# PEER layers as one stage, modulation spread over other stages, attention slots in another order

## What is computed

```python
h = modulate(x, norm_mix_g[l], sh1, sc1)          # RMSNorm, scale, shift
y = mixer_ab(h, ...) if l == 0 else mixer_ssd(h, ...)
x = x + g1 * y
h = modulate(x, norm_ffn_g[l], sh2, sc2)
x = x + g2 * peer_ffn(h, ...)

def peer_ffn(h):                                   # for each token
    q = (h @ wq).reshape(8 heads, 256)             # two halves of 128
    s1, s2 = q[:, :128] @ k1.T, q[:, 128:] @ k2.T  # 128 keys a half
    # top 16 of s1 and of s2, top 16 of their 256 sums -> 16 experts a head
    act = gelu(u_tab[expert] . h);  gate = softmax(best)
    return sum(gate * act * v_tab[expert])         # over 8 heads x 16 experts
```

## Time and profile before

| | us |
|---|---|
| median of 3 runs | 3028.67 |
| lowest, highest | 3025.58, 3033.92 |
| the profiled execution | 3031.45 |
| its span, first to last instruction | 3029.7 |
| PE, DVE busy in it | 2320.6, 1477.1 |
| POOL, ACT busy in it | 905.6, 636.4 |

### The profile page before, as it was taken

How to read it: one execution, slowest core, us unless ns; L and a number is a source line. 1 busy time by engine, 2 the same in 40 slices (tenths; PEclk the granted TensorE clock), 3 DMA queues, 4 the chain that set the end, 5 groups by cost and what they waited for, 6 DMA issues and landing times. The chain is left out here.

```text
span 3029.7 us, 24058 instructions
## 1 busy us (share of the span) xinstructions
PE 2320.6 (77%) x8016; PEld 1271.0 (42%) x8016; DVE 1477.1 (49%) x3612; ACT 636.4 (21%) x1444; POOL 905.6 (30%) x779
## 2 busy tenths in 40 slices
PE   5876678867778777877896879678677877777876
PEld 2543345523333333333675678455433323333333
DVE  0124411177667767763133521411376767766754
ACT  1115412212222222121112211201222222222211
POOL 1203300054444444542002322000144444444441
PEclk8887789989989989998997865589899999999898
DMA  8724627499999999996231034022399999999993
GB/s 330 295 87 188 270 80 291 167 405 421 421 422 421 422 421 422 421 417 266 92 121 52 1 88 120 28 111 85 131 422 421 422 421 421 421 421 421 419 413 159
DMA packets 144208, 860.23 MB, mean 284 GB/s; under 512 B 15133, under 2 KB 39012, under 8 KB 52012
## 3 DMA queue, kind: packets, MB, share of 16 engines
q0 software_dynamic: 101376, 721.47, 57.6%
q1 hardware_dynamic: 42719, 137.37, 12.5%
HBM read 845.65 MB, written 13.18 MB: 283 GB/s over the span
## 5 line engine op out<-in xcount | busy, mean ns | idle before, releaser
L1797 POOL DMA_INDIRECT exp_rows<-in_peer_uv_dram,expert x640 | 738.2, 1153 | 1360.9 <-PE exp_acc L1824 774.8
L1823 PE MATMUL exp_acc<-exp_rows,exp_diag 128*128 128x512 f32 x1280 | 736.4, 659 | 392.5 <-ACT exp_diag L1845 392.4
L1882 DVE CUSTOM_DVE_ANT_0 exp_rows<-exp_rows,htok 128x1024 f32<-128x1024 f32 x640 | 784.6, 1226 | 448.9 <-DMA exp_rows<-in_peer_uv_dram,expert 447.9
L1824 PE MATMUL exp_acc<-exp_rows,exp_diag 128*128 128x512 f32 x1280 | 707.1, 636 | 0.0
L1823 PEld LDWEIGHTS exp_acc<-exp_rows,exp_diag 128*128 128x128 f32 x1280 | 251.6, 207 | 782.0 <-ACT exp_diag L1845 514.4
L1824 PEld LDWEIGHTS exp_acc<-exp_rows,exp_diag 128*128 128x128 f32 x1280 | 263.9, 206 | 346.4 <-issue 346.4
L1840 ACT ACTIVATE exp_act<-exp_dots 128x4 f32<-128x4 f32 x160 | 32.9, 205 | 1235.0 <-DVE exp_dots L1882 1235.0
L1845 ACT ACTIVATE exp_diag<-ident,exp_w 128x128 f32<-128x128 f32 x640 | 204.5, 390 | 36.7 <-DVE exp_w L1887 36.7
L489 PE MATMUL ssd_in_ps<-hT,ssd_in_w 128*128 128x320 f32 x640 | 174.5, 436 | 10.1 <-ACT hT L367 10.1
L489 PE MATMUL peer_q_ps<-hT,peer_q_w 128*128 128x320 f32 x512 | 145.3, 446 | 20.3 <-ACT hT L367 20.3
L489 PEld LDWEIGHTS ssd_in_ps<-hT,ssd_in_w 128*128 128x128 f32 x640 | 122.7, 192 | 62.0 <-ACT hT L367 10.7
(11 more groups left out here) (371 smaller groups left out, 2218.1 us busy)
## 6 DMA issues: line engine op xcount, KB each, us to landing
ada_aw<-in_ada_w_dram SPq DMA_DIRECT2D x12, 2048.0 KB, 7.7
peer_q_aw<-in_ada_w_dram SPq DMA_DIRECT2D x12, 2048.0 KB, 8.1
ssd_in_w<-in_ssd_w_in_dram SPq DMA_DIRECT2D x20, 1024.0 KB, 4.7
peer_q_w<-in_peer_wq_dram SPq DMA_DIRECT2D x16, 1024.0 KB, 6.1
ab_in_w<-in_ab_w_in_dram SPq DMA_DIRECT2D x10, 1024.0 KB, 4.7
exp_rows<-in_peer_uv_dram,expert POOLq DMA_INDIRECT x640, 18.6
out_ssm_sample_dram<-state_hd SPq DMA_DIRECT2D x8, 1024.0 KB, 5.2
ssd_out_w<-in_ssd_w_out_dram SPq DMA_DIRECT2D x4, 2048.0 KB, 7.1
```

Source lines behind the costliest of these rows:

```text
L1797: pool.indirect_dma_start(rows[n % NSLOT][:], None, table, bass.IndirectOffsetOnAxis(ap=experts[:, n:n + 1], axis=0)).then_inc(landed[n % ...
L1823: pe.matmul(acc[t % 2][0][:], d[:], row[:, D:D + 512], start=opens, stop=closes)
L1824: pe.matmul(acc[t % 2][1][:], d[:], row[:, D + 512:2 * D], start=opens, stop=closes).then_inc(mixed, 1)
L1882: dve.tensor_tensor_reduce(u, u, m.htok[:, t, :], 1.0, 0.0, ALU.mult, ALU.add, dots[:, k:k + 1]).then_inc(dotted, 1)
```

## The change

- `stage_peer` replaces peer_q, scores and exp of a layer. It holds the norm, the projection of head j, its scores, and the stream of pairs. Heads 0 to 2 are projected and scored ahead of the stream; in turn j PE does the halves of head j + 3 at pairs 2, 5, 8 and 11 and its scores at pair 13. The token rows of the second prompt tile and of the samples are turned in turns 5 and 6. The keys come in already transposed (`peer_kT`, 1 MB a layer). The sample scores are written straight to their half of the partitions, without the copies `qz` and `hdup`.
- `Ada` takes a list of (layer, part): three parts stay in the first stage, five go beside ab_out's 4 blocks, four beside ssd_in's 20 blocks. Its loops are written out, and `turn` of a step comes after `make` of the next.
- In `stage_attend` a sample unit's scores come after the mix in its own slot, and the orders on ACT and DVE follow.

`stage_scores` and `peer` are deleted; the core of the rest:

```diff
+    def load(self, sp, t):
+        layer, part = self.items[t // 2]
+        if t >= 2:
+            sp.wait_ge(self.made, t - 1)
+        sp.dma_start(self.wt[t % 2][:].rearrange("p c n -> p (c n)"), self.w[layer][:, 2 * part + t % 2, :]).then_inc(self.loaded[t % 2], 16)
...
+                for t in range(ada.steps):
+                    ada.make(pe, t)
+                    if t:
+                        ada.turn(pe, t - 1)
+                ada.turn(pe, ada.steps - 1)
...
                     for n in range(blocks):
+                        if conv and 2 * n >= XC:
+                            for j in range(2):
+                                dve.wait_ge(taken[n % 2], OPEN + n // 2 * 2 + j + 1)
+                                convolve(dve, m, 2 * n + j - XC, tapped)
                         for t in steps(n):
-                            ada.add(dve, t // 2, t % 2)
+                            ada.add(dve, t)
...
+                        ada.make(pe, t)
                         if t:
-                            ada.turn(pe, (t - 1) // 2, (t - 1) % 2)
+                            ada.turn(pe, t - 1)
                 if ada:
-                    ada.turn(pe, Ada.STEPS - 1, 1)
...
                         for t in steps(n):
-                            ada.copy(act, t // 2, t % 2)
+                            ada.copy(act, t)
             else:
+                if ada:
+                    @block.scalar
+                    def _(act):
+                        for t in range(ada.steps):
...
+                            for t in steps(2 * i + k):
+                                ada.add(dve, t)
+                    if ada:
+                        ada.scales(dve)
...
                 pe.wait_ge(qset, 4)
-                scores(*at(0))
-                new_scores(*at(0))
                 for k in range(NU + 3):
+                    if at(k)[0] != "S":
+                        scores(*at(k))
                     fold(*at(k - 3))
-                    turn(*at(k - 2), at(k))
-                    scores(*at(k + 1))
+                    turn(*at(k - 2), at(k - 1))
                     mix(*at(k - 2))
-                    new_scores(*at(k + 1))
+                    if at(k)[0] == "S":
+                        scores(*at(k))
+                        new_scores(*at(k))
...
                 for k in range(NU + 2):
-                    logits(*at(k))
-                    keep(*at(k - 2))
-                    logs(*at(k))
-                    weights(*at(k - 1))
+                    if at(k)[0] == "S":
+                        keep(*at(k - 2))
+                        weights(*at(k - 1))
+                        logits(*at(k))
+                        logs(*at(k))
+                    else:
+                        logits(*at(k))
+                        keep(*at(k - 2))
+                        logs(*at(k))
+                        weights(*at(k - 1))
...
                 for k in range(NU + 3):
-                    mask(*at(k))
-                    place(*at(k - 3))
-                    weights(*at(k - 1))
-                    outputs(*at(k - 2))
+                    if at(k)[0] == "S":
+                        weights(*at(k - 1))
+                        outputs(*at(k - 2))
+                        place(*at(k - 3))
+                        mask(*at(k))
+                    else:
+                        mask(*at(k))
+                        weights(*at(k - 1))
+                        outputs(*at(k - 2))
+                        place(*at(k - 3))
...
+    AHEAD = 3
...
+            @block.sync
+            def _(sp):
+                for j in range(EH):
+                    if j >= 2:
+                        sp.wait_ge(qmade, 2 * j - 2)
+                    sp.dma_start(wt[j % 2][:].rearrange("p c n -> p (c n)"), a["peer_wq"][layer][:, j, :]).then_inc(wloaded[j % 2], 16)
+                    if j == 1:
+                        sp.dma_start(kT[:].rearrange("p h k -> p (h k)"), a["peer_kT"][layer]).then_inc(kloaded, 16)
...
+                def hidden(t):
+                    r = rounds.index(f"h{t}")
+                    for g in range(2):
+                        if r:
+                            pe.wait_ge(tkept, 2 * (r - 1) + g + 1)
+                        for i in range(4):
+                            c = 4 * g + i
+                            if t < 2:
+                                ins = pe.transpose(psT[g][:, i * P:(i + 1) * P], m.hT[:, c, t * P:(t + 1) * P], m.ident[:])
+                            else:
+                                for half in range(2):
+                                    ins = pe.matmul(psT[g][64 * half:64 * half + 64, i * P:(i + 1) * P], m.hT[:, c, TP:T], m.ident[:],
+                                                    start=True, stop=True)
+                        ins.then_inc(tmade, 1)
+                def project(j, side, lo, hi):
...
+                    if lo == 0:
+                        pe.wait_ge(wloaded[j % 2], 16 * (j // 2 + 1))
+                        if j:
+                            pe.wait_ge(qkept, 2 * (j - 1) + side + 1)
+                    for c in range(lo, hi):
+                        ins = pe.matmul(psq[side][:, 0:T], wt[j % 2][:, c, side * P:(side + 1) * P], m.hT[:, c, :],
+                                        start=(c == 0), stop=(c == KC - 1))
+                    if hi == KC:
+                        ins.then_inc(qmade, 1)
...
+                def scores(j):
+                    r = rounds.index(f"s{j}")
+                    pe.wait_ge(kloaded, 16)
+                    pe.wait_ge(qkept, 2 * j + 2)
+                    pe.wait_ge(tkept, 2 * r - 1)
+                    for t in range(2):
+                        for side in range(2):
+                            ins = pe.matmul(psT[0][:, (2 * t + side) * NK:(2 * t + side + 1) * NK], q[j % 2][:, side, t * P:(t + 1) * P],
+                                            kT[:, 2 * j + side, :], start=True, stop=True)
+                    ins.then_inc(tmade, 1)
+                    o = 64 * (j // 4)
+                    pe.wait_ge(tkept, 2 * r)
+                    for side in range(2):
+                        ins = pe.matmul(psT[1][o:o + 64, side * NK:(side + 1) * NK], q[j % 2][:, side, TP:T], kT[:, 2 * j + side, :],
+                                        start=True, stop=True)
+                    ins.then_inc(tmade, 1)
...
+                hidden(0)
+                for j in range(AHEAD):
+                    for side in range(2):
+                        project(j, side, 0, KC)
+                    scores(j)
                 for n in range(pairs):
                     t = tile_of[n // TOPK]
+                    j, at = n // TOPK, n % TOPK
+                    if j + AHEAD < EH:
+                        if at in (2, 5, 8, 11):
+                            side, half = divmod((at - 2) // 3, 2)
+                            project(j + AHEAD, side, 4 * half, 4 * half + 4)
+                        if at == 13:
+                            scores(j + AHEAD)
+                    if at == 3 and j in (EH - AHEAD, EH - AHEAD + 1):
+                        hidden(j - (EH - AHEAD) + 1)
...
             def _(act):
+                def hidden(t):
+                    r = rounds.index(f"h{t}")
+                    for g in range(2):
+                        act.wait_ge(tmade, 2 * r + g + 1)
+                        act.copy(m.htok[:, t, g * 512:(g + 1) * 512], psT[g][:]).then_inc(tkept, 1)
+                def query(j, side):
+                    act.wait_ge(qmade, 2 * j + side + 1)
+                    act.copy(q[j % 2][:, side, :], psq[side][:, 0:T]).then_inc(qkept, 1)
+                def scores(j):
+                    r = rounds.index(f"s{j}")
+                    o = 64 * (j // 4)
+                    act.wait_ge(tmade, 2 * r + 1)
+                    act.copy(m.sc[:, 0:2 * EH * 2 * NK].rearrange("p (t h k) -> p t h k", t=2, h=EH)[:, :, j, :],
+                             psT[0][:].rearrange("p (t k) -> p t k", t=2)).then_inc(tkept, 1)
+                    act.wait_ge(tmade, 2 * r + 2)
+                    act.copy(m.sc[o:o + 64, (2 * EH + j % 4) * 2 * NK:(2 * EH + j % 4 + 1) * 2 * NK], psT[1][o:o + 64, 0:2 * NK]).then_inc(tkept, 1)
...
-                choice.exp(act, 1)
+                norm.scalar(act)
+                hidden(0)
+                for j in range(AHEAD):
+                    for side in range(2):
+                        query(j, side)
+                    scores(j)
+                    if j:
+                        choice.exp(act, j - 1)
...
+                    t, j, at = tile_of[n // TOPK], n // TOPK, i % (TOPK // OCT)
+                    if j + AHEAD < EH:
+                        if at in (1, 2):
+                            query(j + AHEAD, at - 1)
+                        if at == 3:
+                            scores(j + AHEAD)
+                    if at == 1 and j in (EH - AHEAD, EH - AHEAD + 1):
+                        hidden(j - (EH - AHEAD) + 1)
```

(62 more changed lines are left out.)

262 lines of the change are left out of this document (80 added, 182 removed).

## The result

The changed kernel takes 2924.9 us (median of four runs, 2922.9 to 2934.5) against 3029.8 for the kernel before: ratio 0.9661, interval 0.9646 to 0.9676. The time lies inside the range and 21 us above the forecast of 2904. The profiled execution has a span of 2923.0 us.

The account below looks back on a forecast made before the run. Bound by DMA bytes in the expert streams, elsewhere by PE or chains of waits. 3031.45 - 34 - 2 + 36 - 95.6 + 31 - 60.3 = 2906.6, less 2.8 for the median, 2904 us; range 2872 to 2960.

Parts of the forecast that it names:

- First gather: Both PEER layers: first gather 40 us after the norm's first square, against 153.2 and 118.7 before.
- The fourth rival: PEER layers: the gather starts no earlier because the choice still waits for late work; 3061 us in all, chance 0.02.
- The turn: Expert stream, turns with projections: 45 us each, between 41.8 and 48; 8 us starved, a layer 884 us.
- the first rival: Expert stream: ACT's order and the slow clock feed each other, a turn near 50 us; 2954 in all, chance 0.13.
- PE's room in a turn: Expert stream: PE's work is 38.5 us a turn, under the 39.8 of its gathers.
- The sum by the busy column: Expert stream: reckoned by busy time, 32 + 10 us a turn, some 2 over the gathers; 20 in all, 2924.
- ab_out: Stage ab_out with ten modulation steps beside it: +36 us, bounds +29 and +42, loads waiting through two buffers.
- ssd_in: Stage ssd_in with eight modulation steps: +31 us, bounds +26 and +36; four convolutions behind step 6's addition, tail 14.2.
- Attention: Attention stage: page waits go, the sample unit's own chain, 23.4 us a unit, takes over; -2, bounds -11 and +25.
- The second rival: Attention stage: the unit's chain runs at the slow level, 27 us a unit; 2931 in all, chance 0.10.
- First modulation: First stage, six modulation steps instead of twelve: 34 us saved.
- The third rival: Ten new turns of the expert stream: PE stays at 1.2 GHz, 77 us of PE work a turn; 3224, chance 0.03.

Follow-up runs that it names:

- e1: The changed kernel with ACT's copy of query side 1 and the choice's exponential put behind the fourth group's gelu and scalings in turns 0 to 4: 2893.6 us.
- e9: The changed kernel with only the choice's exponential put behind the fourth group's scalings, the copy of query side 1 left ahead of its gelu: 2892.8 us.
- e10: The changed kernel with only the copy of query side 1 put behind the fourth group's scalings, the exponential left behind the third group's: 2892.1 us.
- e7: The changed kernel with all modulation steps in the first stage and none beside ab_out and ssd_in: 2954.5 us.
- e6: The changed kernel with attention's slots put back in the order of before on PE, ACT and DVE: 2932.7 us.

## Why the forecast was right, and where its steps were off

**First gather.** Forecast 40 us after the square in both layers; 41.9 and 39.4. The fourth rival, of a gather that starts no earlier, is out.

**The turn, the step that was mis-sized.** The order of waits was right: ACT at query side 1, table loads, fourth gelu, scores, DVE's first dot. The size was not. The prediction had 38.5 us of PE's work and gaps of 4.3 and 2.5 us, and it priced the slow passes behind these gaps at nothing in the 45, keeping 1.7 us each for the bound. Measured, the gaps are 3.0 and 2.5, and slow passes add 2.0 to 3.6 us a turn to PE's 38.0: turns of about 47.1 where the fourth group's passes were slow too, 45.5 in the one turn of each layer where they were not (two passes behind a gap of 2.48 us took 1.12 us, the next two 1.02). Five turns then lie 35 us behind the bytes' pace instead of 26; by this estimate the slots carried 15 of them, not 18, and starvation went from 8 to 20 us. That is about what the layers missed 884 by, 12.4 and 9.5 us. The mean turn, 46.8, is nearer to the prediction's bound of 48, where both gaps are paid in full, than to its 45; the first rival's turn of 50 was not reached.

**PE's room in a turn.** The step that put PE at 38.5 us a turn, under the 39.8 of bytes, held. Busy time by stretches, a turn of e1 in which every pass ran at full pace, and a turn of the changed kernel:

```profile
647.97:689.02 41.05, 38.02 (x108) 19.54 (x108) 28.30 (x75) 10.40 (x28) 18.01 (x16) 1.00 1.01 421
```

```profile
562.97:610.12 47.15, 41.65 (x108) 21.07 (x108) 27.98 (x75) 10.42 (x27) 18.67 (x16) 0.93 1.01 421
```

The same 108 instructions keep PE busy for 38.0 us at a granted clock of 1.00 and for 41.7 at 0.93, so the busy column counts slow passes as work and does not by itself say whether a turn fits. Here the trace agrees with the Trainium skill ("Trainium Kernel Development and Optimization", Performance Expectations), which calls matmul busy time a bad metric. The sum by the busy column, 2924 us, is the measured time almost to the microsecond, but by chance: e1, e9 and e10 leave PE's work in a turn as it is and win over 30 us.

**ab_out.** +42 against +36, at the upper bound. The walk had the wait for step 4 (3.4 forecast, 3.77 measured) and missed the same wait for step 9, 3.38, and the slow passes behind both. With a third buffer it is +29.3, the lower bound.

**ssd_in.** +27.5 against +31: four convolutions do stand behind the addition of step 6, but the tail was 11.2 us instead of 14.2, because a convolution followed the one before it every 1.9 us where the earlier trace rows had shown 2.4 with its waits. It takes 2.0 in e7 too, where no modulation stands beside ssd_in, so its waits went with the new code of the loop and not by the modulation.

**Attention.** -3.7 against -2: as forecast, the waits for pages went and the unit's chain, 20.5 to 23.6 us from the end of one unit's scores to that of the next, took over. That the gain came out of shorter passes and not out of less waiting (e6) was not forecast. The second rival (27 us a unit) did not come, although the stretch's clock is 0.73.

**First modulation.** -37 against -34, in an execution in which this stage was as short as in any run with two buffers.

**The third rival.** A granted clock under 0.8 in the turns was to decide for it; it was 0.91 to 0.93.

**The sum.** The terms miss in both directions: the two layers and ab_out are together 28 us longer than forecast, the other stages some 10 shorter. That the time is off by 21 us and not by more is in part luck.

## What to carry to other kernels

When work is folded into a stream that another resource paces, write down the closed loop of waits through the in-order queues, with each idle gap's slow passes priced in, and compare it with the pacing resource's time; a sum of busy times says only that it could fit. What lags per turn times the number of turns is free up to what the slots hold, and every microsecond beyond is paid, so taking out any one link can be worth all of it. And a wait removed is worth only the distance to the next one: 42 us of PE's waits for pages were replaced by 56 us of others, and the 3 us won came from passes that ran faster.

## What was not expected of the hardware

The same gap does not always cost the same. In the changed kernel PE idles 2.47 or 2.48 us ahead of the fourth group in all ten turns with projections; its next four passes are slow in eight of them (2.5 to 3.6 us together) and at full pace in two (2.0), the third turn of each layer. In e1, with only the gap ahead of the first group left, ten such gaps (3.0 us, once 3.4) are followed by slow passes among the next four in seven cases. A slow pass takes about twice as long, which fits the two levels of 1.2 and 2.4 GHz; idle time alone does not decide between them, and the runs don't show what did. The same unsteadiness reaches a whole stage: the first modulation, with the same code, took 40.7 us in the changed kernel, where the last product and the two turns behind it took 1.92, 1.06 and 1.03 us, and 44.2 in e9, where they took 3.64, 1.88 and 1.85. So this stage cannot be compared between two runs to better than these 4 us by one execution each.
